# Two Transformer-style blocks in one kernel: identity turns at the start, four stages written in another order, the zero keys of four attention windows cut, and a split last store

## The chip, the cores and the metric

The kernel runs on one core of one Trainium2 chip. A core has TensorE (PE; its weight loads are shown as PEld), VectorE (DVE), ScalarE (ACT), GpSimd (POOL) and SyncE (SP, which only issues DMAs here). The time is device microseconds (us) of one execution, as the median over several executions; less is better. TensorE's clock has two levels, 1.2 and 2.4 GHz, and the profile's column PEclk says which share of 2.4 GHz was granted.

## The reference

Two blocks run one after the other on x of [1, 512, 1024] in float32. Cut to what matters:

```python
# first block
h = rms_norm(x, ln1_g);  z = h @ w_in            # 1024 -> 6656 columns
a = gelu(z_a); u, v = split(a)
v = layer_norm(v)                                 # over 512, with gain and bias
y_a = (u * chunked_spatial_gating(v, sg_w, sg_b)) @ w_a_out
c = p * sigmoid(g_lin)
c = causal_depthwise_conv(c, cv_w, cv_b)          # 31 taps, 512 channels
c = silu(layer_norm(c, cv_ln_g, cv_ln_b));  y_b = c @ w_b_out
y_c = stick_breaking_attention(q, k, vv) @ w_c_out   # 8 heads of 64
merged = gates[0] * y_a + gates[1] * y_b + gates[2] * y_c
x = x + merged @ w_out
up = causal_depthwise_conv(rms_norm(x, ln2_g) @ w_up, ffn_conv_w, ffn_conv_b)
x = x + (silu(gate) * val) @ w_down
# second block: a gated linear recurrence beside sliding-window attention
# (16 query heads, 4 key heads, window 128, blocks of 128, sinks; for the first
# block of queries the block of keys before it is all zeros and masked out)
merged = sigmoid(m_rnn) * (y_rnn @ w_rnn_out) + sigmoid(m_attn) * (y_attn @ w_attn_out)
x = x + merged @ w_o
out = rms_norm(x, final_norm_g)
```

## The kernel before, in words

Weights arrive on SP's queue in transfers of 1 MB into two STAGE buffers. Each transfer holds two "units". For a unit, ACT writes the rounded high part (`hi`, L585, WH) and DVE the rest (`lo`, L1030, WL), both in the format fp32r, into a ring of four slots; an activation is split the same way (XH, XL). A product is three matmuls of 512 columns, high by high, high by low, low by high, and a unit is 24 of them. PE takes the units in order (`unit(n)` waits for `hi_done` and `lo_done`); `hi(n + 4)` waits until PE is done with unit n. Every engine's program is one list written out by hand, and semaphores join the lists; PE, ACT and DVE each work strictly in order.

The places that this change touches, in order of time:

- **Start** (SP L430 to L441, ACT L605 to L620, DVE L1054 to L1085, PE L1749 to L1783). x comes in four token tiles (XTOK). PE turns each with 8 transposes into PSUM; DVE multiplies by the gain (`x_gain`, XG, L1058), ACT rounds (`x_high`, XH, L612) and copies (`x_copy`, XCM, L606), and DVE subtracts (`x_low`, XL, L1066). Unit 0 then goes over the four token tiles, unit 1 after it.
- **Second stage, units U_B** (DVE L1152 to L1262, PE L1842 on). DVE normalises the gate values VSG in four groups of three instructions (L1156 to L1161). After that it drains PSUM for unit i (`CPAD`, `TG`, L1239), and PE's unit i + 2 waits for the drain of unit i. Between the units PE does the steps of the stick-breaking attention (`stick_pe`), for which DVE does `pair_mask` (L1212) and `pair_scan` (L1225). The 124 instructions of the depthwise convolution (`taps`, CACC, L1180 and L1184) are dealt out over DVE's list.
- **Gate units of the last branch, `gates_first`** (p = 0 to 7; DVE L1303 to L1357, PE L1899 to L1917). DVE adds the four parts of CACC (L1319 to L1321, `c_sum`), and PE forms the mean with ONES after unit p = 2. Mean, variance, root and product follow, until BH and BL are there for the two "quad" units, which fill four PSUM banks. DVE then merges bank by bank (L1352, L1355).
- **Output projection, units U_D** (PE L1938 to L1944). The first unit waits for each of the eight parts MH and ML of the merged sum.
- **Windows of the second block** (PE L2056 to L2084, DVE L1517 on, ACT L863 and L874). 16 windows, each of 256 keys for 128 queries; for the windows with w % 4 == 0 the first 128 keys are zeros.
- **End** (DVE L1665 to L1677, SP L476 to L480): per token tile a drain, the sum of squares, a root, a reciprocal, one product over 1024 columns and one store of 512 KB.

## Time and profile before

| | us |
|---|---|
| median of 3 runs (lowest, highest) | 1326.31 (1323.57, 1326.85) |
| the profiled execution | 1323.74 |
| its span | 1321.8 |
| PE busy | 1298.2 (98%) |
| DVE busy | 844.5 (64%) |
| ACT busy | 609.5 (46%) |
| all DMA queues | 128.73 MB, mean 97 GB/s |

The span runs from the first to the last instruction that the profiler saw. In a row of the timeline the first number is the start in us from the span's start and the second the length; a matmul's length reaches over the next one's start, since matmuls are pipelined, so the distance between two starts is what one costs. The bracket at the end of a row is the idle time of that engine ahead of it and what ended it.

### The profile page before, as it was taken

To read this page: it belongs to the slowest core of one execution; us is meant where nothing else is said; L and a number is where in the kernel's file an instruction comes from. 1 tells how busy PE (TensorE), PEld (TensorE's weight loads), DVE (VectorE), ACT (ScalarE), POOL (GpSimd) and SP (SyncE) were. 2 spreads that over 40 slices of the span, in tenths; PEclk is the share of its full clock that TensorE was granted. 3 is DMA by queue.
4 is the path that set the end of the run, shared out by engine and by line. 5 is a ranking of instruction groups with operands and counts; after the bars stand their busy time and mean duration, and the time that the engine had idled before them with its cause. 6 is when DMAs were issued, how large, how long until landed. Compare 5 with 4: busy or idle time off the path is not lost.

```text
span 1321.8 us, 15645 instructions
## 1 busy us (share of the span) xinstructions
PE 1298.2 (98%) x5991; PEld 1046.0 (79%) x5991; DVE 844.5 (64%) x1110; ACT 609.5 (46%) x886; POOL 85.6 (6%) x70
## 2 busy tenths in 40 slices
PE   7999999999999999999999999999999999999997
PEld 6887777788777888888888888887877777778886
DVE  5458789889976776666665335435368878445534
ACT  6234467232263443333343224423389999544232
POOL 0000222000000200000000002100012220000000
PEclk9999999999999999999999999999999999999999
DMA  7432111422322322222222222422312221214211
GB/s 235 184 103 68 64 64 65 155 75 89 97 94 76 116 96 95 95 95 95 95 95 96 95 95 94 162 96 96 96 64 87 73 80 65 96 64 159 96 64 64
DMA packets 98282, 128.73 MB, mean 97 GB/s; under 512 B 2952, under 2 KB 80688, under 8 KB 97712
## 3 DMA queue, kind: packets, MB, share of 16 engines
q1 hardware_dynamic: 98208, 127.93, 28.7%
q8 instruction: 39, 0.64, 0.2%
q14 instruction: 19, 0.16, 0.0%
q10 hardware_dynamic: 16, 0.00, 0.0%
HBM read 121.63 MB, written 6.29 MB: 97 GB/s over the span
## 4 chain that ended last, share of the span: by engine, by line
PE 90%; DVE 7%; ACT 2%; DMA 1%; issue 1%; SPq 0%; DVEq 0%; ACTq 0%
PE PS L1683 87%; PE PS L1750 3%; DVE WL L1030 1%; ACT WH L585 1%; DMA STAGE<-in_w_in 1%; DVE QK L1132 0%; DVE CACC L1184 0%; DVE XL L1066 0%; DVE XG L1058 0%; DMA LNR<-in_ln_g 0%; DVE VSG L1160 0%; DVE MERG L1294 0%; DVE MERG L1355 0%; DVE MERG L1369 0%; DVE TMPY L1352 0%
## 5 line engine op out<-in xcount | busy, mean ns | idle before, releaser
L585 ACT ACTIVATE WH<-STAGE 128x1024 fp32r<-128x1024 f32 x214 | 225.8, 1057 | 489.5 <-PE PS L1683 473.6
L1030 DVE TENSOR_TENSOR WL<-STAGE,WH 128x1024 fp32r<-128x1024 f32 x214 | 276.3, 1293 | 228.3 <-ACT WH L585 227.8
L1683 PE MATMUL PS<-XH,WH 128*128 128x512 f32 x960 | 383.5, 399 | 2.4 <-DVE CPAD L1239 2.4
L1683 PE MATMUL PS<-XH,WL 128*128 128x512 f32 x960 | 375.6, 391 | 0.0
L1683 PE MATMUL PS<-XL,WH 128*128 128x512 f32 x960 | 375.4, 391 | 0.0
L1683 PEld LDWEIGHTS PS<-XH,WH 128*128 128x128 f32 x960 | 181.1, 189 | 45.1 <-issue 4.6
L1683 PEld LDWEIGHTS PS<-XL,WH 128*128 128x128 f32 x960 | 181.3, 189 | 38.7 <-issue 2.4
L1683 PEld LDWEIGHTS PS<-XH,WL 128*128 128x128 f32 x960 | 181.0, 189 | 38.3
L1683 PE MATMUL PS<-WH,XH 128*128 128x512 f32 x224 | 88.3, 394 | 1.1 <-DVE XL L1066 1.1
L1683 PE MATMUL PS<-WL,XH 128*128 128x512 f32 x224 | 87.3, 390 | 0.0
L1683 PE MATMUL PS<-WH,XL 128*128 128x512 f32 x224 | 87.3, 390 | 0.0
L1184 DVE SCALAR_TENSOR_TENSOR CACC<-CPAD,VEC,CACC 128x512 f32<-128x512 f32 x120 | 84.3, 760 | 0.1
L1403 DVE TENSOR_TENSOR UPB<-PS,RBC 128x512 f32<-128x512 f32 x44 | 30.3, 689 | 70.7 <-PE PS L1683 70.6
L1683 PE MATMUL PS<-FL,WH 128*128 128x512 f32 x176 | 68.5, 389 | 0.0
L1683 PE MATMUL PS<-FH,WH 128*128 128x512 f32 x176 | 68.5, 389 | 0.0
L1683 PE MATMUL PS<-FH,WL 128*128 128x512 f32 x176 | 68.5, 389 | 0.0
L510 POOL TENSOR_TENSOR SS<-SS,SQ 128x512 f32<-128x512 f32 x16 | 22.7, 1419 | 580.7 <-ACT SQ L594 580.7
L1683 PEld LDWEIGHTS PS<-WH,XH 128*128 128x128 f32 x224 | 42.2, 188 | 10.9 <-issue 1.1
L1683 PEld LDWEIGHTS PS<-WL,XH 128*128 128x128 f32 x224 | 42.2, 188 | 8.7 <-issue 0.2
L1683 PEld LDWEIGHTS PS<-WH,XL 128*128 128x128 f32 x224 | 42.1, 188 | 8.9
L791 ACT ACTIVATE YB<-UPB,VEC 128x512 f32<-128x512 f32 x44 | 35.3, 803 | 12.1 <-DVE UPB L1403 12.1
L1683 PEld LDWEIGHTS PS<-FH,WH 128*128 128x128 f32 x176 | 33.0, 188 | 6.9
(298 smaller groups left out, 1840.1 us busy)
## 6 DMA issues: line engine op xcount, KB each, us to landing
STAGE<-in_w_in SPq DMA_DIRECT2D x52, 1024.0 KB, 4.9
STAGE<-in_w_up SPq DMA_DIRECT2D x22, 1024.0 KB, 5.0
STAGE<-in_w_down SPq DMA_DIRECT2D x11, 1024.0 KB, 4.8
STAGE<-in_w_out SPq DMA_DIRECT2D x4, 1024.0 KB, 4.8
STAGE<-in_w_rnn_out SPq DMA_DIRECT2D x4, 1024.0 KB, 4.9
STAGE<-in_w_attn_out SPq DMA_DIRECT2D x4, 1024.0 KB, 4.7
STAGE<-in_w_o SPq DMA_DIRECT2D x4, 1024.0 KB, 4.9
XTOK<-in_x SPq DMA_DIRECT2D x4, 512.0 KB, 6.1
```

What stands on the lines that cost most here:

```text
L510: pool.tensor_tensor(SS[:], SS[:], SQ[:], ALU.add).then_inc(ss_added, 1)
L585: act.activation(ring(WH, n), staged(n), ACT.Copy).then_inc(hi_done, 1)
L791: act.activation(YB[:, r, :], UPB[:, r, 4:516], ACT.Identity, scale=VEC[:, bass.ds(V_FW[2] + c, 1)], bias=VEC[:, bass.ds(V_FB + c, 1)]).th ...
L1030: dve.tensor_tensor(ring(WL, n), staged(n), ring(WH, n).bitcast(F32), ALU.subtract)\
L1184: ins = dve.scalar_tensor_tensor(CACC[:, c, :], CPAD[:, c, 2 + j:2 + j + SEQ], col(V_CVW + KW * j + c), CACC[:, c, :], ALU.mult, ALU.add)
L1403: dve.tensor_tensor(UPB[:, r, 4:516], PS[:, r, :], RBC[:], ALU.mult)\
L1683: return pe.matmul(out_, lhsT, rhs, start=start, stop=stop, skip_group_check=True)
L1750: return pe.transpose(out_, in_, IDENT[:])
```

## The change

The list of changes, with where each stands:

1. Start: SP asks for x tile 0, then the first weights, then tiles 1 to 3. PE turns the identity 10 times before the gain row's transpose and 14 times between tile 0 and tile 1 (into a bank that nobody reads), turns tile 3 between unit 0 and unit 1 of tile 0, and does units 0 and 1 together for each token tile. ACT and DVE take the weights' parts ahead of the tiles' parts.
2. Second stage: the first drain stands ahead of the gate normalisation, which is dealt out in pairs of groups around the second drain; `pair_mask(0)` comes one step earlier. From i = 6 on a step has 4 taps in place of 3, and the last taps come earlier.
3. `gates_first`: sum, mean, squares, variance, root and product each stand one p earlier. The second quad unit goes bank by bank with a signal for each, and DVE merges on these signals, with `lo(U_D + 1)` behind the merges.
4. The first two units of the output projection are interleaved in halves of four parts.
5. Windows with w % 4 == 0 leave the 128 zero keys out of scores, mask, maximum, exponential, scaling, transposes and copy.
6. End: the left half is multiplied by the gain ahead of time and scaled by ACT, the right half by DVE, and each half is stored by itself.

The diff, cut:

```diff
+def first_key(w):
+
+    return 0 if w % TT else P
...
-            for t in range(2):
-                sp.dma_start(XTOK[:, t, :], xt[:, t, :]).then_inc(x_in[t], 16)
+            sp.dma_start(XTOK[:, 0, :], xt[:, 0, :]).then_inc(x_in[0], 16)
             for p, src in enumerate(transfers()):
                 kd, ncol = src.shape[1], src.shape[2]
                 if p == 1:
-                    for t in range(2, TT):
+                    for t in range(1, TT):
                         sp.dma_start(XTOK[:, t, :], xt[:, t, :]).then_inc(x_in[t], 16)
...
+            hi(0)
             x_high(0)
             x_copy(0)
-            hi(0)
+            hi(1)
             x_high(1)
             x_copy(1)
-            hi(1)
             x_high(2)
...
+            lo(0)
+            x_low(0)
             x_gain(1)
-            x_low(0)
-            lo(0)
+            lo(1)
             x_low(1)
             x_gain(2)
             x_gain(3)
             x_low(2)
...
-            dve.wait_ge(vg_sd, 1)
-            sd = SMALL[:, S_LN + 40:S_LN + 44]
-            link(dve.reciprocal(sd, sd))
-            for tt in range(TT):
+            def gate_norm(tt):
+                sd = SMALL[:, S_LN + 40:S_LN + 44]
+                if tt == 0:
+                    dve.wait_ge(vg_sd, 1)
+                    link(dve.reciprocal(sd, sd))
...
-            tap_order = [(c, j) for j in range(12) for c in (0, 1)]
-            tap_order += [(c, j + (12 if c < 2 else 0)) for j in range(CVK - 12) for c in range(KW)]
-            tap_order += [(c, j) for j in range(CVK - 12, CVK) for c in (2, 3)]
+            tap_order = [(c, j) for j in range(15) for c in (0, 1)]
+            tap_order += [(c, j + (15 if c < 2 else 0)) for j in range(CVK - 15) for c in range(KW)]
+            tap_order += [(c, j) for j in range(CVK - 15, CVK) for c in (2, 3)]
...
+                if i < 2:
+                    gate_norm(2 * i)
+                if i == 1:
+                    pair_mask(0)
+                if i < 2:
+                    gate_norm(2 * i + 1)
...
-                if 1 <= i < 13:
+                if 2 <= i < 13:
...
-                    taps(3)
+                    taps(3 if i < 6 else 4)
...
-                        taps(4)
-
+                        taps((4, 4, 4, 4, 6, 3)[r])
+
+            assert taps_done == KW * CVK
             for p in range(10):
-                dve.wait_ge(unit_done, U_C + 24 + p + 1)
+                if p < 9:
...
                 if p == 0:
-                    taps(4)
-                    assert taps_done == KW * CVK
-                if p == 1:
                     dve.wait_ge(c_tap, KW * CVK)
...
-                if p == 2:
+                if p == 1:
...
                 if p == 9:
                     for m in range(4):
+                        if m < 3:
+                            dve.wait_ge(quad_done, m + 1)
+                        else:
+                            dve.wait_ge(unit_done, U_C + 34)
                         dve.wait_ge(gs_ready, 16 + m + 1)
...
+            lo(U_D + 1)
             for m in range(4):
                 merged_low(m)
 
             for m in range(4):
                 if m < 3:
-                    dve.wait_ge(quad_done, m + 1)
+                    dve.wait_ge(quad_done, 3 + m + 1)
...
-                mask = AM[:, 1:3, :] if nb else AM[:, 0:3:2, :]
+                kb = first_key(w) // P
                 for par in range(2):
-                    dve.tensor_tensor(buf[:, par].rearrange("p i (b c) -> p i b c", b=2),
-                                      PS[:, 6 + par, :].rearrange("p (i b c) -> p i b c", i=2, b=2),
-                                      mask.unsqueeze(1).broadcast_to([P, 2, 2, P]),
+                    dve.tensor_tensor(buf[:, par].rearrange("p i (b c) -> p i b c", b=2)[:, :, kb:],
+                                      PS[:, 6 + par, :].rearrange("p (i b c) -> p i b c", i=2, b=2)[:, :, kb:],
+                                      AM[:, kb:, :].unsqueeze(1).broadcast_to([P, 2, 2 - kb, P]),
                                       ALU.add).then_inc(s2_mask, 1)
...
                 dve.wait_ge(s2_mask, 2 * w + 2)
-                link(dve.tensor_reduce(att(w, 0).rearrange("p (a b) -> p a b", a=2), buf[:], AX.X, ALU.max))
+                link(dve.tensor_reduce(att(w, 0).rearrange("p (a b) -> p a b", a=2),
+                                       buf[:, :, :, kb * P:], AX.X, ALU.max))
...
+                dve.wait_ge(fin_sq, t + 1)
+                v = XT2[:, t, 0:512]
+                dve.tensor_tensor(v, v, FG[:, 0:512], ALU.mult).then_inc(fin_gain, 1)
+            for t in range(TT):
...
-                link(dve.reciprocal(s_, s_))
-                dve.scalar_tensor_tensor(XT2[:, t, :], XT2[:, t, :], s_, FG[:], ALU.mult, ALU.mult)\
+                dve.reciprocal(s_, s_).then_inc(fin_rcp, 1)
+                dve.wait_ge(fin_rcp, t + 1)
+                dve.scalar_tensor_tensor(v, v, s_, FG[:, 512:1024], ALU.mult, ALU.mult)\
                    .then_inc(fin_ready, 1)
...
+            def turn_identity(n):
+
+                for _ in range(n):
+                    tr(PS[:, 6, 0:P], IDENT[:])
+
+            def x_turn(t):
...
+            pe.wait_ge(consts, 2)
+            turn_identity(10)
+            pe.wait_ge(ln_in, 16)
+            tr(PS[:, 7, 0:P], LNR[:]).then_inc(ln_t, 1)
+            x_turn(0)
+            turn_identity(14)
+            x_turn(1)
+            x_turn(2)
...
+            def first_units(t):
+                first_tile(t)
+                ts = slice(t * P, (t + 1) * P)
+                for n in (U_A, U_A + 1):
+                    if t == 0:
+                        unit(n)
+                        if n > U_A:
+                            x_turn(3)
+                    for k in range(2):
+                        kk = 2 * (n - U_A) + k
+                        last = split_mm(PS[:, t, :], XH[:, kk, ts], XL[:, kk, ts],
+                                        ring(WH, n)[:, k, :], ring(WL, n)[:, k, :], kk == 0, False)
+                    if t == TT - 1:
+                        last.then_inc(unit_done, 1)
+
+            for t in range(TT):
+                first_units(t)
 
...
-                    if p == 2:
+                    if p == 1:
                         pe.wait_ge(c_sum, 1)
                         pe.wait_ge(drained, DR_C + 32)
                         mm(PS[:, 4, :], ONES[:], TG1[:], True, True).then_inc(c_mean, 1)
-                    if p == 4:
+                    if p == 3:
                         pe.wait_ge(c_ssum, 1)
                         mm(PS[:, 5, :], ONES[:], TG0[:], True, True).then_inc(c_var, 1)
                 pe.wait_ge(c_cent, KW)
...
-                for u in range(2):
-                    quad_unit(U_C + 32 + u, u, 4, BH, BL, KW)
+                quad_unit(U_C + 32, 0, 4, BH, BL, KW)
+                n = U_C + 33
+                unit(n)
+                for m in range(4):
+                    for k in range(2):
+                        last = split_mm(PS[:, 4 + m, :], ring(WH, n)[:, k, m * P:(m + 1) * P],
+                                        ring(WL, n)[:, k, m * P:(m + 1) * P], BH[:, 2 + k, :],
+                                        BL[:, 2 + k, :], False, k == 1)
+                    last.then_inc(quad_done if m < 3 else unit_done, 1)
...
+            for h in range(2):
+                for m in range(2):
+                    if h == 0:
+                        pe.wait_ge(drained, DR_D - 7 + m)
+                        unit(U_D + m)
+                    for k in range(4 * h, 4 * h + 4):
+                        if m == 0:
+                            pe.wait_ge(mh_ready, k + 1)
+                            pe.wait_ge(ml_ready, k + 1)
+                        last = split_mm(PS[:, 4 + m, :], ring(WH, U_D + m)[:, k, :],
+                                        ring(WL, U_D + m)[:, k, :], MH[:, k, :], ML[:, k, :],
+                                        k == 0, k == KD - 1)
+                    if h:
+                        last.then_inc(unit_done, 1)
+            for m in range(2, KD):
                 pe.wait_ge(drained, DR_D - 7 + m if m < 4 else DR_D + m - 3)
-
-                def ready(k):
-                    pe.wait_ge(mh_ready, k + 1)
-                    pe.wait_ge(ml_ready, k + 1)
-                cm_unit(U_D + m, 4 + m % 4, MH, ML, 0, ready if m == 0 else None)
-
+                cm_unit(U_D + m, 4 + m % 4, MH, ML)
...
-                        last = mm(PS[:, 6 + par, idx * 256:idx * 256 + 256],
+                        last = mm(PS[:, 6 + par, idx * 256 + first_key(w):idx * 256 + 256],
                                   Q2T[rows_, 2 * g + idx, nb * P:(nb + 1) * P],
-                                  K2T[rows_, g, nb * P:nb * P + 256], True, True)
+                                  K2T[rows_, g, nb * P + first_key(w):nb * P + 256], True, True)
                 last.then_inc(qk2_done, 1)
...
-                for kb in range(2):
+                for kb in range(first_key(w) // P, 2):
...
+                        act.wait_ge(fin_rcp, t + 1)
+                        act.wait_ge(fin_gain, t + 1)
+                        act.activation(XT2[:, t, 0:512], XT2[:, t, 0:512], ACT.Copy,
+                                       scale=SMALL[:, S_FIN + t:S_FIN + t + 1]).then_inc(fin_left, 1)
...
+                sp.wait_ge(fin_left, t + 1)
+                sp.dma_start(ot[:, t, 0:512], XT2[:, t, 0:512]).then_inc(stored, 16)
                 sp.wait_ge(fin_ready, t + 1)
-                sp.dma_start(out.rearrange("o (t p) d -> p (o t) d", p=P)[:, t, :], XT2[:, t, :])\
-                  .then_inc(stored, 16)
-            sp.wait_ge(stored, 16 * TT)
+                sp.dma_start(ot[:, t, 512:1024], XT2[:, t, 512:1024]).then_inc(stored, 16)
```

PE's list at its beginning: before, and then of the change. XTOK are the x tiles, LNR the gain row, and the rows of WH, WL with XH, XL are unit 0.

```order
L1750 MATMUL PS<-IDENT,LNR 128x128
L1750 MATMUL PS<-IDENT,XTOK 128x128 x32
L1683 MATMUL PS<-WH,XH 128x512
L1683 MATMUL PS<-WL,XH 128x512
L1683 MATMUL PS<-WH,XL 128x512
```

```order
L1778 MATMUL PS<-IDENT 128x128 x10
L1778 MATMUL PS<-IDENT,LNR 128x128
L1778 MATMUL PS<-IDENT,XTOK 128x128 x8
L1778 MATMUL PS<-IDENT 128x128 x14
L1778 MATMUL PS<-IDENT,XTOK 128x128 x16
L1711 MATMUL PS<-WH,XH 128x512
L1711 MATMUL PS<-WL,XH 128x512
L1711 MATMUL PS<-WH,XL 128x512
```

The last 8 transposes of x moved behind the first six matmuls, and 24 turns of the identity are new.

DVE's list where the second stage begins: before, and then of the change. VSG are the gate values, CPAD the drains of units U_B + 0 and U_B + 1.

```order
L1150 TENSOR_SCALAR SMALL<-SMALL 128x4
L1154 RECIPROCAL SMALL<-SMALL 128x4
L1156 TENSOR_SCALAR VSG<-VSG,SMALL 128x512
L1160 TENSOR_TENSOR VSG<-VSG,SGLN 128x512
L1161 TENSOR_TENSOR VSG<-VSG,SGLN 128x512
...
L1161 TENSOR_TENSOR VSG<-VSG,SGLN 128x512
L1239 TENSOR_TENSOR CPAD<-PS,RBC 128x512
L1030 TENSOR_TENSOR WL<-STAGE,WH 128x1024
L1239 TENSOR_TENSOR CPAD<-PS,RBC 128x512
```

```order
L1160 TENSOR_SCALAR SMALL<-SMALL 128x4
L1250 TENSOR_TENSOR CPAD<-PS,RBC 128x512
L1166 RECIPROCAL SMALL<-SMALL 128x4
L1167 TENSOR_SCALAR VSG<-VSG,SMALL 128x512
L1171 TENSOR_TENSOR VSG<-VSG,SGLN 128x512
L1172 TENSOR_TENSOR VSG<-VSG,SGLN 128x512
...
L1172 TENSOR_TENSOR VSG<-VSG,SGLN 128x512
L1040 TENSOR_TENSOR WL<-STAGE,WH 128x1024
L1250 TENSOR_TENSOR CPAD<-PS,RBC 128x512
```

The first drain moved ahead of all twelve VSG instructions, the second ahead of six of them.

DVE's list at the end of the taps: before, and then of the change, from the last MERG row on. CACC x4 are taps, GS drains of the units p = 0 and 1, and the two TG names the sum that PE's mean needs.

```order
L1294 TENSOR_TENSOR MERG<-MERG,TMPY 128x512
L1184 SCALAR_TENSOR_TENSOR CACC<-CPAD,VEC,CACC 128x512 x4
L1311 TENSOR_TENSOR GS<-PS,RBC 128x512
L1030 TENSOR_TENSOR WL<-STAGE,WH 128x1024
L1184 SCALAR_TENSOR_TENSOR CACC<-CPAD,VEC,CACC 128x512 x4
L1311 TENSOR_TENSOR GS<-PS,RBC 128x512
L1030 TENSOR_TENSOR WL<-STAGE,WH 128x1024
L1319 TENSOR_TENSOR TG_77<-CACC 128x512
L1320 TENSOR_TENSOR TG_94<-CACC 128x512
L1321 TENSOR_TENSOR TG_77<-TG_77,TG_94 128x512
```

```order
L1311 TENSOR_TENSOR MERG<-MERG,TMPY 128x512
L1330 TENSOR_TENSOR GS<-PS,RBC 128x512
L1040 TENSOR_TENSOR WL<-STAGE,WH 128x1024
L1336 TENSOR_TENSOR TG_77<-CACC 128x512
L1337 TENSOR_TENSOR TG_94<-CACC 128x512
L1338 TENSOR_TENSOR TG_77<-TG_77,TG_94 128x512
```

Eight taps, one drain and one WL row no longer stand between the last merge and the sum.

## Rows read from the trace of the kernel before

**Rows 1.** Waits of PE: what waited for what, us in total, times, longest.

```profile
PE PS L1683 <- DVE TG L1321: 2.8, 1, 2.8
PE PS L1683 <- ACT MH L769: 2.8, 3, 1.0
PE PS L1683 <- DVE CPAD L1239: 2.4, 1, 2.4
PE PS L1683 <- DVE XL L1066: 1.1, 2, 0.6
PE PS L1683 <- ACT II L905: 0.8, 1, 0.8
```

**Rows 2.** Timeline of the start, PE and DVE.

```profile
9.81 0.48 PE L1750 MATMUL PS<-IDENT,XTOK 128*128 128x128 f32 x1 [1.52 <-DMA XTOK<-in_x]
13.14 0.75 PE L1683 MATMUL PS<-WH,XH 128*128 128x512 f32 x1
19.42 2.36 DVE L1030 TENSOR_TENSOR WL<-STAGE,WH 128x1024 fp32r<-128x1024 f32 x2 [0.40 <-ACT WH L585]
```

**Rows 3.** The first weight transfer, issued at 1.71: time to landing.

```profile
DMA to landing us min/median/max: 6.8/6.8/6.8
```

**Rows 4.** Busy time by stretch: start:end length, PE, PEld, DVE, ACT, POOL, PEclk, DMA share, GB/s.

```profile
9.80:13.10 3.30, 3.29 (x16) 3.29 (x17) 3.08 (x3) 3.30 (x5) 0.00 (x0) 1.00 1.04 384
122.90:126.40 3.50, 3.49 (x8) 2.84 (x9) 3.50 (x5) 0.00 (x0) 0.00 (x0) 0.51 0.00 0
364.57:372.00 7.43, 7.43 (x26) 5.80 (x25) 3.52 (x5) 3.08 (x5) 0.00 (x0) 0.77 0.24 90
```

**Rows 5.** Timeline where the second stage begins, PE and DVE.

```profile
114.31 0.18 DVE L1154 RECIPROCAL SMALL<-SMALL 128x4 f32<-128x4 f32 x1 [1.80 <-ACT SMALL L661]
122.17 0.68 DVE L1239 TENSOR_TENSOR CPAD<-PS,RBC 128x512 f32<-128x512 f32 x1
122.91 0.79 PE L1683 MATMUL PS<-XH,WH 128*128 128x512 f32 x1 [2.43 <-DVE CPAD L1239]
```

**Rows 6.** Waits of DVE from 128 to 240 us, as in rows 1.

```profile
DVE TG L1239 <- PE PS L1683: 6.3, 4, 3.3
DVE WL L1030 <- ACT WH L585: 5.7, 11, 1.3
```

**Rows 7.** Timeline around the sum of the convolution, ACT, DVE and PE.

```profile
344.95 1.06 ACT L585 ACTIVATE WH<-STAGE 128x1024 fp32r<-128x1024 f32 x1 [4.38 <-PE PS L1683]
350.39 1.06 ACT L585 ACTIVATE WH<-STAGE 128x1024 fp32r<-128x1024 f32 x1 [4.38 <-PE PS L1683]
353.05 2.74 DVE L1184 SCALAR_TENSOR_TENSOR CACC<-CPAD,VEC,CACC 128x512 f32<-128x512 f32 x4
360.10 0.68 DVE L1311 TENSOR_TENSOR GS<-PS,RBC 128x512 f32<-128x512 f32 x1
364.01 1.13 PE L1683 MATMUL PS<-TG,ONES 128*128 128x512 f32 x2 [2.84 <-DVE TG L1321]
```

**Rows 8.** Timeline of PE at the first unit of the output projection.

```profile
420.71 0.39 PE L1683 MATMUL PS<-MH,WL 128*128 128x512 f32 x1
422.10 0.47 PE L1683 MATMUL PS<-MH,WH 128*128 128x512 f32 x1 [1.00 <-ACT MH L769]
```

**Rows 9.** Timeline of PE: a window's transposes and scores, with the rows behind them.

```profile
1120.56 1.03 PE L1750 MATMUL PS<-IDENT,S2A 128*128 128x128 f32 x8
1121.35 0.48 PE L1683 MATMUL PS<-BHR,WH 128*128 128x512 f32 x1
...
1128.00 1.14 PE L1683 MATMUL PS<-K2T,Q2T 64*128 64x256 f32 x8
1129.07 0.50 PE L1683 MATMUL PS<-BHR,WH 128*128 128x512 f32 x1
```

**Rows 10.** The end on DVE, and the last store's time to landing.

```profile
1317.51 1.28 DVE L1676 SCALAR_TENSOR_TENSOR XT<-XT,SMALL,FG 128x1024 f32<-128x1024 f32 x1
...
DMA to landing us min/median/max: 2.6/2.6/2.6
```

More of the change, by code:

```diff
@@ L529, in _ @@
             pool.wait_ge(unit_done, U_G)
-            pool.memset(AM[:, 0, :], -BIG).then_inc(gchain, 1)
-            pool.memset(AM[:, 1:3, :], 0.0).then_inc(gchain, 1)
-            n += 2
+            pool.memset(AM[:], 0.0).then_inc(gchain, 1)
+            n += 1
             pool.wait_ge(gchain, n)
-            pool.affine_select(out=AM[:, 1, :], in_=AM[:, 1, :], compare_op=ALU.is_gt, fill=-BIG,
+            pool.affine_select(out=AM[:, 0, :], in_=AM[:, 0, :], compare_op=ALU.is_gt, fill=-BIG,
                                base=0, pattern=[[1, P]], channel_multiplier=-1).then_inc(consts, 1)
-            pool.affine_select(out=AM[:, 2, :], in_=AM[:, 2, :], compare_op=ALU.is_ge, fill=-BIG,
+            pool.affine_select(out=AM[:, 1, :], in_=AM[:, 1, :], compare_op=ALU.is_ge, fill=-BIG,
                                base=0, pattern=[[-1, P]], channel_multiplier=1).then_inc(consts, 1)
-            pool.memset(K2T[:, :, 0:P], 0.0).then_inc(consts, 1)
             pool.memset(UP2[:, :, 0:4], 0.0).then_inc(consts, 1)
@@ L1081, in _ @@
             x_low(2)
-            lo(1)
             x_low(3)
@@ L1750, in tr @@
                 return pe.transpose(out_, in_, IDENT[:])
-            pe.wait_ge(consts, 2)
-            pe.wait_ge(ln_in, 16)
-            tr(PS[:, 7, 0:P], LNR[:]).then_inc(ln_t, 1)
-            for t in range(TT):
+            def turn_identity(n):
+                for _ in range(n):
+                    tr(PS[:, 6, 0:P], IDENT[:])
+            def x_turn(t):
                 pe.wait_ge(x_in[t], 16)
```

41 lines of the change are left out of this document (24 added, 17 removed).

## The prediction, made before the kernel was run

> **What bounds the kernel now.** I read the page first: PE is busy for 1298.2 of 1321.8 us, and no other engine is above 64%. So only PE's 23.6 us of idle time, the time it runs below full clock, and work taken off its list can be worth anything. The waits of PE come next [rows 1]: 2.8 us for the sum TG, 2.8 us in three pieces for MH, 2.4 us for the drain CPAD, 1.1 us for XL and 0.8 us for II; the reader is to see that each is one place, not a pattern. Then the timeline at those places, for what the wait is made of, and the busy time by stretch [rows 4] for the clock: behind the waits for CPAD and TG the granted clock is 0.51 and 0.77, so each of them is followed by matmuls at the lower of the two levels, 1.2 GHz. What a wait costs is its length and that stretch together.
>
> Two prices recur. A unit of 24 matmuls at full clock takes 5.44 us, the distance of the two WH rows that each follow a finished unit [rows 7]; that is 0.227 us per matmul. A transpose takes (1121.35 - 1120.56)/8 = 0.10 us there [rows 9], but (13.14 - 9.81)/16 = 0.21 us at the start [rows 2].
>
> **The change part by part.**
>
> *Start.* The column PEclk says 1.00 for 9.80 to 13.10 [rows 4], yet the 16 transposes in it go at 0.21 us, half the pace of those at 1120 us; so PE starts at the lower level and the column does not show it. The Trainium skill warns of this (TensorE: Matmul & The Clock Gate, section "Seeing it yourself"): the clock's trace events have been seen to be unreliable and should be cross-checked against durations. The rows bear that out, and by the column alone the identity turns could gain nothing.
>
> Before, the first matmul starts at 13.14 [rows 2]. Units 0 and 1 are 48 matmuls or 10.9 us; with the waits for XL, 1.1 us, and the slow first matmuls and restarts, about 0.9, unit 1 ends at 26.0. After, the first weights stand ahead of x tile 1. They were issued at 1.71 and landed 6.8 later, at 8.5 [rows 3]; tile 2, the 0.5 MB right behind, let PE go at 9.81 [rows 2], so 0.5 MB is 1.3 us, and the weights land at 7.2. The 10 turns fill PE from about 1.6 to 3.7, tile 0 is turned when it is there, as before, and the 14 turns take 3.0 us slow or 1.4 fast, to 9.4 at the latest, which delays tile 1 (there at 8.5) by at most 0.9 us. From there DVE sets the pace, with ten operations of about 1.15 us from start to start (two WL take 2.36 [rows 2], and XG and XL have as many elements). ACT: WH 7.2 to 8.3, XH to 9.3, XCM to 10.3. DVE: WL 8.4 to 9.5, XL to 10.7. PE starts unit 0 at 10.75, does six matmuls, turns tile 3 and waits for the WL of unit 1 at 13.0. XL of tile 2 comes at 17.7, and from there PE has two tiles of 24 matmuls in all: 17.7 + 5.44 = 23.2. The gain is 26.0 - 23.2 = 2.8 us. Bounds: 0 if the ten DVE operations in the new order take as long as before, 3.5 if PE never waited behind 10.75 (10.75 + 10.9 + 0.9 for tile 3). I take 2.8.
>
> *Second stage.* PE is done with the scores at 122.91 - 2.43 = 120.48 and waits 2.43 us, since DVE drains CPAD at 122.17, behind the twelve VSG operations [rows 5]. Then 8 matmuls take 3.5 us [rows 4] where 1.8 would do: 1.7 lost. After, both drains come sooner: the first ahead of the root's wait, the second at 119.5, behind two groups of (122.17 - 114.31)/4 = 1.97 us and one WL. PE needs only the first. The saving is 2.43 + 1.7 = 4.1 us; I take 4.0, since the first matmul behind an attention step is a little slow at any clock. What is late next: from 114.31 DVE needs four groups, a drain of 0.68, a mask of the same size and a WL of 1.15 until the last VSG, 124.7, and 1.3 for WT, 126.0; PE asks for both after its unit and the next scores, 120.48 + 5.44 + 0.9 = 126.8. It fits with 0.8 us to spare. Six steps then have one tap more, 6 x 0.69 = 4.1 us (a row of four taps is 2.74 [rows 7]). DVE's own waits in that stretch, 6.3 + 5.7 us over eleven steps [rows 6], cover it; when the cover is gone PE waits. Bounds 0 and 4.0; I take 4.0.
>
> *The sum.* PE starts p = 0 at 344.7 and has finished p = 1 two units later, at 355.6 [rows 7]. DVE ends the merges at 353.05. From the drain at 360.10 to PE's start at 364.01 it needs 3.91 us for drain, WL and three additions [rows 7]; the same after 353.05 gives 356.96. So a wait of 1.4 us stays where 3.0 was (with the restart), a gain of 1.6. Behind the wait of 2.84 us, 24 matmuls take 7.43 us at 0.77 [rows 4], 2.0 more than 5.44. Waits of 1.00 us do not bring the clock down [rows 8], one of 2.43 does [rows 5]; 1.4 is nearer to the first. I take 1.6 + 1.9 = 3.5; bounds 1.6 and 4.9. The rest of the chain (squares, variance, root) moves with the sum, and PE asks for BL six units later, as it did five units later before, so nothing is late there.
>
> *Output projection.* The three waits are 2.8 us [rows 1]; between 420.71 and 422.10 is 1.39 for one matmul of 0.23, so a wait of 1.00 costs 1.16 [rows 8], and the three 3.3. After, the second unit's first half gives 12 matmuls, 2.7 us, of work that needs only parts 0 to 3, and DVE's merges start about 4 us sooner. All 3.3 goes. The WL that now stands behind the merges is ready at about 410, and PE needs it at 419. Bounds 2.8 and 3.3.
>
> *Windows.* Four of sixteen lose half their columns. Transposes: 4 of 8, 0.40 of 0.79 us. Scores: the eight rows of 256 columns take 1.07 us (1128.00 to 1129.07) [rows 9]; half the columns can save at most 0.53 and at least 0, and I take 0.45, near the half, as the columns of the transposes are paid in full. That is 4 x 0.85 = 3.4 us off PE's list. The wait of 0.8 for II [rows 1] ends a chain through window 0's mask, maximum, exponentials and copy, all halved, by some 2 us in sum; PE comes 0.85 sooner, so the wait goes too: 4.2. Bounds 0.8 (the scores save nothing and the chain does not move) and 4.5. The mask's and the memset's work on POOL was hidden and is worth nothing.
>
> *End.* Half the columns are scaled on DVE while ACT does the rest: 1.28 becomes about 0.7 [rows 10], and the copy that the store needs is 256 KB instead of 512, against a second issue on SP. The last landing took 2.6 us [rows 10]. I take 0.6; bounds 0.2 and 1.2. The Trainium skill (DMA: Bandwidth & Descriptors, "Anatomy of one DMA") gives about 2.0 us plus the bytes by 436 GB/s, measured on GpSimd's path: estimated by it, 3.2 for the old store, more than the 2.6 here, and 0.6 less for the half. With 0.3 for the product and the issues, the end would gain 0.9 by it instead of 0.6.
>
> **Sum**: 2.8 + 4.0 + 3.5 + 3.3 + 4.2 + 0.6 = 18.4 us. The profiled execution had 1323.74 (span 1321.8 and 1.9 around it), so one like it would have 1305.3. It lies near the lowest of the runs, 1323.57; the median is 2.6 above it. I expect the median in the middle of such a spread, 1.3 above: **1306.6**.
>
> **The rivals.**
> - *The clock falls again behind the 1.4 us.* For it: 2.43 was enough. Against: three waits of about 1 us within 5 us were not. Then 1.9 more: 1308.5.
> - *DVE falls behind in the second stage.* It is nearly full there, and the extra taps are 4.1 us. If its own waits do not cover them, PE's scores wait for the sigmoid, which waits for DVE's mask, and the 4.0 is given back: 1310.6.
> - *The start gives nothing*, as DVE's ten operations, or the weights' landing, set the end of unit 1: 1309.4.
> - *It becomes slower.* One mechanism: with PE 4 us sooner, each of the ten steps from 130 to 215 us ends in a wait for DVE's mask. Small waits add; from 18.4/10 = 1.8 us a step on, all is lost, and waits of that size are near the 2.43 that brought the clock down for 1.6. With 2.4 + 1.6 at each of ten steps, 40 us, it would be 1346; with waits of 2.1 us alone, 1328. Against it: DVE has about 1.1 us of its own waits in a step now [rows 6], and no wait of PE stands in that stretch [rows 1].
> - *The change does not do what it says*: the identity turns end before the clock rises. They cost nothing then, since they lie in waits for the DMAs; that is within the start's bounds.
>
> **How the numbers follow.** Forecast 0.60; clock again 0.13; DVE behind 0.11; start gives nothing 0.10; smaller misses of several terms together, near 1312 to 1318, 0.03; slower 0.03. The range 1302 to 1313 holds the first four with their spread; the lower end is the upper bounds of start, sum, windows and end (0.7 + 1.4 + 0.3 + 0.6 more) with the spread's 1.3. A measurement here tells 0.3%, 4.0 us, from no change, that is below 1322.3 for faster. Only the last two cases come near it: faster 0.96, same 0.02, slower 0.02.
>
> **What would show it.** In the profile after: PE's first matmul of unit 0 near 10.8 and the end of unit 1 near 23; no wait for CPAD and a clock of 1.00 in the stretch behind; a wait for TG of about 1.4 with the clock still at 1.00; no waits for MH; scores of window 0 in about 0.6 instead of 1.07 and no wait for II; two stores per tile, and a last product of 0.69 us. A new line of PE waiting for ACT's GB or BT between 120 and 220 us would prove the forecast wrong, as would a median above 1313.

## The result, and the profile after

The change took 17.1 us off the median: 1307.83 us (1307.77 to 1308.16, four runs) against 1324.94 (1323.45 to 1326.85, four runs of the kernel before beside it), a ratio of 0.9871 with a 95% interval of 0.9857 to 0.9884. I had forecast 1306.6 in a range of 1302 to 1313. The profiled execution of the changed kernel took 1308.16 with a span of 1306.4; the one of before took 1323.74 with 1321.8. So from profile to profile 15.6 us went, 15.4 of them in the span, where my sum had 18.4.

First line of part 1 of the changed kernel's page, and then its waits of PE (what waited for what, us in total, times, longest):

```profile
PE 1292.2 (99%) x5999; PEld 1042.2 (80%) x5999; DVE 842.0 (64%) x1114; ACT 608.1 (47%) x890; POOL 85.3 (7%) x68
```

```profile
PE PS L1778 <- POOL ONES L504: 1.6, 1, 1.6
PE PS L1711 <- DVE TG L1338: 1.2, 1, 1.2
PE PS L1711 <- ACT BT L677: 0.9, 1, 0.9
PE PS L1778 <- DVE KDUP L1522: 0.8, 1, 0.8
PE PS L1778 <- ACT AT L686: 0.8, 1, 0.8
PE PS L1711 <- ACT II L911: 0.5, 1, 0.5
```

Of the five waits in [rows 1], MH, CPAD and XL are gone, TG fell from 2.8 to 1.2 and II from 0.8 to 0.5. Two are new, for BT and for AT, both in the second stage: the line of which I had said that it would prove the forecast wrong. It did so for one step of it. (The 1.6 for ONES is the start: PE now waits for the identity and then turns it, in the time in which it waited 4.4 us for the gain row LNR before.)

What each place gave is read from the start of one and the same PE instruction in both timelines. Before, at six places:

```profile
53.77 0.59 PE L1683 MATMUL PS<-SS,ONES 128*128 128x512 f32 x1
141.16 0.70 PE L1683 MATMUL PS<-QKT 64*128 64x512 f32 x2
220.87 0.38 PE L1750 MATMUL PS<-IDENT,BT 128*128 128x128 f32 x2
416.47 0.39 PE L1683 MATMUL PS<-MH,WH 128*128 128x512 f32 x1
469.13 0.59 PE L1683 MATMUL PS<-SS,ONES 128*128 128x512 f32 x1
1314.79 0.39 PE L1683 MATMUL PS<-WH,M2L 128*128 128x512 f32 x1
```

And after, the same six:

```profile
51.20 0.59 PE L1711 MATMUL PS<-SS,ONES 128*128 128x512 f32 x1
134.49 0.70 PE L1711 MATMUL PS<-QKT 64*128 64x512 f32 x2
216.10 0.30 PE L1778 MATMUL PS<-IDENT,BT 128*128 128x128 f32 x1 [0.76 <-ACT AT L686]
408.50 0.39 PE L1711 MATMUL PS<-MH,WH 128*128 128x512 f32 x1
457.46 0.59 PE L1711 MATMUL PS<-SS,ONES 128*128 128x512 f32 x1
1299.36 0.39 PE L1711 MATMUL PS<-WH,M2L 128*128 128x512 f32 x1
```

The lead is 2.57, then 6.67, 4.77, 7.97, 11.67 and 15.43 us (at the last matmul), and at the span's end 15.4. The steps between are what each place gave:

| place | forecast | from trace to trace |
|---|---|---|
| start | 2.8 | 2.57 |
| second stage, drains first | 4.0 | 4.10 |
| the same stage, up to 216 us | 0 | -1.90 |
| the sum | 3.5 | 3.20 |
| output projection | 3.3 | 3.70 |
| windows, with the wait for II | 4.2 | 3.76 |
| end | 0.6 | 0.0 |
| in all | 18.4 | 15.4 |

At the two places where the clock was low before [rows 4], the busy time by stretch of the changed kernel (us, then busy us of PE, PEld, DVE, ACT, POOL with their instructions, PEclk, DMA share, GB/s) has it at full level; PE's wait ahead of the second was 1.25 us:

```profile
117.90:121.40 3.50, 3.50 (x18) 2.90 (x17) 3.36 (x7) 1.99 (x3) 0.00 (x0) 1.00 0.00 0
352.10:359.60 7.50, 7.40 (x31) 5.80 (x32) 4.87 (x8) 3.81 (x7) 0.00 (x0) 1.00 0.42 142
```

In windows with w % 4 == 0 the transposes and the scores are about halved; the rows of window 0 and of window 4 after, against the full ones in [rows 9] (eight transposes in 0.79 from start to start, eight scores in 1.07):

```profile
954.07 0.60 PE L1778 MATMUL PS<-IDENT,S2A 128*128 128x128 f32 x4
994.55 0.72 PE L1711 MATMUL PS<-K2T,Q2T 64*128 64x128 f32 x8
```

The row of eight full scores in [rows 9] has a length of 1.14, so halving the columns took 0.42 off; my 0.45 was near.

### The profile page after: what moved, and what is told of

Same layout as the page of the kernel before. It is cut to its first block, busy times and chain, and to the rows that moved or that the text cites. A ratio compares the mean times of both kernels' runs of the same rounds, so it can differ in the third digit from the quotient of the medians.

```text
span 1306.4 us, 15673 instructions
## 1 busy us (share of the span) xinstructions
PE 1292.2 (99%) x5999; PEld 1042.2 (80%) x5999; DVE 842.0 (64%) x1114; ACT 608.1 (47%) x890; POOL 85.3 (7%) x68
## 4 chain that ended last, share of the span: by engine, by line
PE 91%; DVE 5%; ACT 2%; DMA 1%; issue 1%; SPq 0%; ACTq 0%; DVEq 0%
PE PS L1711 88%; PE PS L1778 3%; DVE WL L1040 1%; ACT WH L590 1%; DMA STAGE<-in_w_in 1%; DMA XTOK<-in_x 1%; DVE QK L1142 0%; DVE CACC L1195 0%; DVE RS L1236 0%; DVE MERG L1311 0%; DVE TMPY L1307 0%; DVE VATT L1124 0%; DVE UC L1572 0%; DVE VSG L1124 0%; ACT BT L677 0%
## 5 line engine op out<-in xcount | busy, mean ns | idle before, releaser
L1040 DVE TENSOR_TENSOR WL<-STAGE,WH 128x1024 fp32r<-128x1024 f32 x214 | 280.3, 1312 | 217.2 <-ACT WH L590 216.6
L1711 PEld LDWEIGHTS PS<-FL,WH 128*128 128x128 f32 x176 | 33.0, 188 | 6.9
```

The lines of the kernel that those rows point to most:

```text
L1040: dve.tensor_tensor(ring(WL, n), staged(n), ring(WH, n).bitcast(F32), ALU.subtract)\
L1711: return pe.matmul(out_, lhsT, rhs, start=start, stop=stop, skip_group_check=True)
```

## The experiments

Times are medians; the changed kernel itself gave 1307.83 on one chip and 1307.92 (1307.82 to 1308.05) on another, beside the last three kernels. Its expectation there was:

> The changed kernel itself, beside the next three on one chip: 1307.8, spread under 1 us, while the kernel before spreads over 3 us.

That held. The kernel before gave 1324.8 to 1325.5 beside all of them, spread over 3.1 to 3.8 us. Ratios are to it. "Less" and "more" are against 1307.83 for the changed kernel, and against 1307.92 for the three kernels that ran beside its second measurement. From trace to trace the start alone moves by up to 0.6 us, with the arrival of the first data, so a lead read at one place holds only when the lead ahead of it is taken off.

**Who fills VectorE in the second stage.** The wait for BT (longest 0.95 in its row at 205.65) means that ACT had not read the scores out of PSUM; ACT waited for DVE's mask, and the mask stood behind a long WL. Four experiments.

*Taps back.*

```diff
-                    taps(3 if i < 6 else 4)
+                    taps(3)
-                        taps((4, 4, 4, 4, 6, 3)[r])
+                        taps(((4, 4, 4, 4, 6, 3) if b + q == 0 else (5, 5, 5, 5, 6, 3))[r])
```

> The changed kernel, but with 3 taps in every step from i = 4 on, as before, and the six moved taps dealt out one at a time over the units of the later quads of the third stage. Theory (the added taps fill VectorE): the two new waits of TensorE, for BT at 205.7 us (0.95) and for AT at 216.1 us (0.76), which cost 1.11 + 0.92 = 2.0 us, go, and the last scores before 217 us start 2.0 us earlier, 1307.8 - 2.0 = 1305.8. Rival (the waits come from TensorE being 4.1 us earlier than before, and VectorE and GpSimd are in each other's way whatever the taps): the waits stay, 1307.8.

1306.31 (1306.19 to 1306.63), 1.5 us less; ratio 0.9856 (0.9841 to 0.9871). The wait for BT is gone, that for AT is 0.4 instead of 0.8. By 216 us the trace is 1.10 earlier although its start was 0.27 later, so the stage gave 1.4. That is most of the loss of 1.9, and not all: between the theory and its rival. What is left has a cause of its own, in the step ahead of the wait (DVE, then POOL):

```profile
206.57 2.36 DVE L1210 TENSOR_TENSOR UU<-UU,TG 128x512 f32<-128x512 f32 x1 [0.16 <-ACT TG L716]
```

```profile
206.56 1.82 POOL L531 TENSOR_TENSOR BT<-BT,RS 128x768 f32<-128x768 f32 x1 [5.86 <-DVE RS L1236]
```

UU<-UU,TG takes 0.66 in the same step of the changed kernel. Here it is 1.7 longer, ACT's WH waits 2.42 for it, and WL, mask and sigmoid come behind WH. The next experiments show what stretches it.

*Drains alone.* The kernel before with this and the rest of that stage's edit:

```diff
                 dve.tensor_tensor(dst, PS[:, i % 2, :], RBC[:], ALU.mult).then_inc(drained, 1)
+                if i < 2:
+                    gate_norm(2 * i)
```

> The kernel before with only the change to the drains, the gate normalisation and the first mask of the second stage. Theory (taps fill VectorE): with 3 taps a step the whole 4.1 us of the CPAD wait and the low clock behind it is kept, 1324.9 - 4.1 = 1320.8, and TensorE waits for neither BT nor AT. Rival (TensorE's lead is the cause): 2.0 of it is given back, 1322.9, with the two waits of some 0.8 us there.

1320.90 (1318.48 to 1323.04, nine runs), ratio 0.9968 (0.9958 to 0.9978), 4.6 us less than before. In the trace it is 4.1 (3.5 earlier at 141 us, from a start that was 0.6 later), and no wait of PE at all between 117 and 230 us. With three taps a step the whole 4.1 stays. The rival falls.

*Mask first.* What is long about WL? DVE's timeline in a step of the changed kernel, then POOL's:

```profile
182.40 0.66 DVE L1250 TENSOR_TENSOR TG<-PS,RBC 128x512 f32<-128x512 f32 x1
182.99 2.53 DVE L1040 TENSOR_TENSOR WL<-STAGE,WH 128x1024 fp32r<-128x1024 f32 x1
185.44 0.42 DVE L1223 TENSOR_TENSOR PS<-PS,MMIN 128x256 f32<-128x256 f32 x1
```

```profile
182.62 1.82 POOL L531 TENSOR_TENSOR BT<-BT,RS 128x768 f32<-128x768 f32 x1 [6.52 <-DVE RS L1236]
```

WL takes 1.22 where nothing runs beside it, and here 2.53: of the 1.45 us that it lies beside POOL's product it lost 1.31. The scan that ends ahead of the drain releases the product, so in the four steps from 174 to 203 us the WL starts beside it. The Trainium skill has this (GPSIMD Engine Reference, section "Specifications"): GpSimd's way into SBUF is shared with VectorE, and they contend where a VectorE instruction has two SBUF inputs. The trace agrees, and also where one input is in PSUM: the drain beside it keeps its 0.66.

Which of the two loses goes by which began first. In the rows above the product was there first, in those of the taps' experiment by 0.01 us, and VectorE lost. At 208.92 of the changed kernel VectorE was first:

```profile
208.92 0.66 DVE L1210 TENSOR_TENSOR UU<-UU,TG 128x512 f32<-128x512 f32 x1
```

```profile
209.14 2.15 POOL L531 TENSOR_TENSOR BT<-BT,RS 128x768 f32<-128x768 f32 x1 [6.52 <-DVE RS L1236]
```

Here UU keeps its 0.66, and the product takes 2.15 instead of 1.82. In the trace of the drains alone both begin at 209.42; UU takes 0.69 and the product 2.38. So the last step of that trace was spared the collision that the taps' experiment has. The experiment moves WL:

```diff
-                lo(U_B + i + 4)
+                if i < 6:
+                    lo(U_B + i + 4)
                 if 2 <= i < 13:
                     pair_mask(i - 1)
                 tg_mult(i - 1)
+                if i >= 6:
+                    lo(U_B + i + 4)
```

> The changed kernel, but from i = 6 on VectorE's subtraction WL stands behind the mask and the gate product instead of ahead of them. Theory (VectorE is full, and its operations that read two SBUF operands run at about half pace while GpSimd's product BT<-BT,RS runs): the PSUM drain and the mask then lie beside GpSimd's product, WL takes 1.2 to 1.9 us instead of 2.5 to 2.7, the mask comes over 1 us earlier in each step, and the waits for BT and AT go: 1307.8 - 1.9 = 1305.9. Rival (the mask now waits for the scores, and VectorE stands idle ahead of it): nothing gained, 1307.8 or up to 1 us more.

1306.00 (1305.84 to 1306.20), 1.8 us less, with all the added taps in place; ratio 0.9855 (0.9839 to 0.9872). Both waits are gone. The same step, DVE and then POOL:

```profile
181.74 0.67 DVE L1250 TENSOR_TENSOR TG<-PS,RBC 128x512 f32<-128x512 f32 x1
182.32 0.42 DVE L1223 TENSOR_TENSOR PS<-PS,MMIN 128x256 f32<-128x256 f32 x1
182.65 1.68 DVE L1210 TENSOR_TENSOR UU<-UU,TG 128x512 f32<-128x512 f32 x1
184.25 1.21 DVE L1040 TENSOR_TENSOR WL<-STAGE,WH 128x1024 fp32r<-128x1024 f32 x1
```

```profile
181.96 1.82 POOL L531 TENSOR_TENSOR BT<-BT,RS 128x768 f32<-128x768 f32 x1 [6.19 <-DVE RS L1236]
```

Drain and mask, which work on PSUM, pass beside the product at their own pace. VectorE's UU<-UU,TG, both inputs in SBUF, takes the collision (1.68 instead of 0.68), and a WL of 1.21 follows. The mask starts 0.58 us behind the drain's start instead of 3.04, and with it the sigmoids.

*Half of POOL's product.* Half of the products BT<-BT,RS is left out, the four taps stay.

```diff
-                pool.tensor_tensor(b, b, RS[:, :, 0:STEP_W[s % 3]], ALU.mult).then_inc(a_ready, 1)
+                b, rs = b[:, 0], RS[:, 0, 0:STEP_W[s % 3]]
+                pool.tensor_tensor(b, b, rs, ALU.mult).then_inc(a_ready, 1)
```

> The changed kernel, with GpSimd's product BT<-BT,RS of the stick-breaking steps over one of its two halves; the other half of the products is left out. Its 4 taps per step stay. Theory (GpSimd's product stretches VectorE's WL): the WL beside it falls from 2.5 to about 1.9 us, the waits for BT and AT go or shrink to under 0.5 us in sum, 1306.1. Rival (WL is long for a reason of its own, the taps alone fill VectorE): WL stays at 2.5, and the waits stay, 1307.8.

1306.16 (1305.90 to 1306.24), 1.7 us less; ratio 0.9856 (0.9839 to 0.9872). DVE's WL, then POOL's product in that step:

```profile
182.28 1.73 DVE L1041 TENSOR_TENSOR WL<-STAGE,WH 128x1024 fp32r<-128x1024 f32 x1
```

```profile
181.93 1.00 POOL L532 TENSOR_TENSOR BT<-BT,RS 128x384 f32<-128x384 f32 x1 [6.53 <-DVE RS L1237]
```

With POOL at 1.00, WL loses 0.5, and both waits are gone. So the cause is shown from both sides: the taps and the collision together fill DVE, and taking away either one brings most of the loss back.

**The turns of the identity.**

```diff
-            turn_identity(10)
...
-            turn_identity(14)
```

> The changed kernel without the 24 turns of the identity. Theory (the turns raise the clock): the transposes of tiles 1 and 2 and the first matmuls go at 0.21 and 0.45 us instead of 0.10 and 0.23; tile 2 is turned 1.0 us later, the six first matmuls take 1.3 more, the third turn of x 0.8 more; with what VectorE's pace hides of it, unit 1 ends 1.5 to 3 us later: 1309.3 to 1310.8. Rival (VectorE's ten operations alone set the start): no change, 1307.8.

1308.47 (1308.19 to 1308.64), 0.55 to 0.64 more than the changed kernel; ratio 0.9873 (0.9858 to 0.9888). PE's timeline without the turns, and then with them:

```profile
8.40 3.57 PE L1778 MATMUL PS<-IDENT,XTOK 128*128 128x128 f32 x16 [1.78 <-DMA XTOK<-in_x]
11.73 0.48 PE L1711 MATMUL PS<-WH,XH 128*128 128x512 f32 x1
12.04 0.40 PE L1711 MATMUL PS<-WL,XH 128*128 128x512 f32 x1
```

```profile
8.53 1.09 PE L1778 MATMUL PS<-IDENT,XTOK 128*128 128x128 f32 x8 [0.37 <-DMA XTOK<-in_x]
9.81 1.09 PE L1778 MATMUL PS<-IDENT,XTOK 128*128 128x128 f32 x8 [0.19 <-DMA XTOK<-in_x]
11.05 0.47 PE L1711 MATMUL PS<-WH,XH 128*128 128x512 f32 x1
```

The turns do raise the clock: tiles 1 and 2 go at half the price, and the first matmul starts 0.68 earlier. Then the changed kernel waits 0.40 before tile 3, and without turns the matmuls are at full level almost at once, so behind tile 3 only 0.13 of it is left. My expectation of 1.5 to 3 us is refuted, and its rival is nearly right. By this pair of traces the turns gave 0.1 us, by the medians, on different chips, about 0.6; the other 2.0 to 2.4 of the start's 2.6 us are the order of tiles and weights.

**The sum ahead of the last merges.** DVE's three additions, moved in front of the four merges of the last quad:

```diff
+                        if r == 5 and b == 1 and q == 1:
+                            dve.wait_ge(c_tap, KW * CVK)
+                            link(dve.tensor_tensor(TG1[:], CACC[:, 0, :], CACC[:, 1, :], ALU.add))
...
                         if r == 5:
                             for m in range(4):
```

> The changed kernel, with the three additions of the convolution's parts ahead of the last four merges instead of behind them, the first drain and a WL. Theory (the wait of 1.25 us for TG is the length of what stands on VectorE between the merges and the sum): it goes with its restart, 1307.8 - 1.4 = 1306.4, and no wait of TensorE takes its place, since the merges, 2 us later, free their banks ahead of the mean. Rival (TensorE then waits for the merges, which free bank 4): the wait changes its name and half of it or all stays, 1307.1 to 1307.8.

1306.51 (1306.43 to 1306.65), 1.3 less; ratio 0.9859 (0.9842 to 0.9875). No wait for TG is left, the mean starts at 350.92 instead of 352.20, and nothing took its place. So the wait lay in what VectorE had to do ahead of the sum, the last merges, one drain and one WL, and the merges themselves can wait.

**The output projection.** Two experiments. First PE's interleaving of units alone taken back:

```diff
-            for h in range(2):
-                for m in range(2):
...
+            for m in range(KD):
+                pe.wait_ge(drained, DR_D - 7 + m if m < 4 else DR_D + m - 3)
...
+                cm_unit(U_D + m, 4 + m % 4, MH, ML, 0, ready if m == 0 else None)
```

> The changed kernel, with the first two units of the output projection one after the other as before, while the merges bank by bank stay. Theory (the signals per bank are what took the waits for MH away; VectorE has the last low part at 412.5 us, and TensorE would ask for it at 413.3): no change, 1307.8. Rival (the interleaving is needed): waits for MH of 0.5 to 2 us in sum come back, 1308.3 to 1310.

1308.16 (1308.00 to 1308.44), ratio 0.9871 (0.9855 to 0.9888), with no wait of PE between 380 and 460 us. The interleaving is worth at most 0.3 us. Then the signals per bank taken back as well, and with them the place of one WL, which stands ahead of the merges again:

```diff
-                        if m < 3:
-                            dve.wait_ge(quad_done, m + 1)
-                        else:
-                            dve.wait_ge(unit_done, U_C + 34)
                         dve.wait_ge(gs_ready, 16 + m + 1)
...
-            lo(U_D + 1)
             for m in range(4):
                 merged_low(m)
```

> The changed kernel with the merges at p = 9 without signals per bank, the WL of U_D + 1 ahead of them, and the first two projection units one after the other, all as before. Theory (the waits for MH cost their length and restart, and at times the clock falls behind them, which is a part of the 3 us by which the kernel before spreads): three waits for MH of 2.1 to 2.8 us in sum, +3.3 to +3.8, so a median of 1311.1 to 1311.6 with single runs up to 2 us above. Rival (the waits cost 3.3 and never touch the clock; the spread of before comes from the waits for CPAD and TG alone): 1311.1 with a spread under 0.7 us.

1312.25, 4.3 us more, with runs at 1311.59, 1311.77, 1312.73 and 1313.72; ratio 0.9902 (0.9887 to 0.9917). The profiled one was the slowest. Its PE, and the stretch behind:

```profile
412.23 0.47 PE L1704 MATMUL PS<-MH,WH 128*128 128x512 f32 x1 [0.80 <-ACT MH L774]
414.16 0.75 PE L1704 MATMUL PS<-MH,WH 128*128 128x512 f32 x1 [1.00 <-ACT MH L774]
414.71 0.63 PE L1704 MATMUL PS<-ML,WH 128*128 128x512 f32 x1
415.14 0.63 PE L1704 MATMUL PS<-MH,WL 128*128 128x512 f32 x1
```

```profile
416.30:422.00 5.70, 5.70 (x16) 4.46 (x17) 4.52 (x6) 3.80 (x5) 0.64 (x1) 0.59 0.25 79
```

From 414.16 on a matmul costs 0.43 instead of 0.23. These are the waits that in the trace of before, with 0.81 and 1.00, left the clock alone [rows 8]. The trace of the drains alone shows the fall too: behind its waits of 0.80 and 1.01 for MH the matmuls from 417 to 423 us cost 0.43. And the other way round: in that same trace the wait of 2.84 us for TG, as long as in [rows 7], is followed by the full level, where [rows 4] has 0.77. PE's row and its stretch there:

```profile
360.46 1.12 PE L1690 MATMUL PS<-TG,ONES 128*128 128x512 f32 x2 [2.84 <-DVE TG L1328]
```

```profile
361.00:371.00 10.00, 10.00 (x45) 8.10 (x44) 6.92 (x11) 4.77 (x7) 0.00 (x0) 1.00 0.23 78
```

So whether the clock falls behind such waits differs between executions. A single wait of 1.25 us for TG, which ten of the traces have, cost no clock in any of them. All kernels that still have the waits for MH or CPAD spread over 2.1 to 4.6 us; the others, ten kernels with four or five runs each, over at most 0.7. The rival, that the waits for MH never touch the clock, is refuted. The signals per bank were not tried apart from the place of that WL: of the 5.5 us by which the merges start later without them (400.24 for 394.74), the WL is 1.15.

**The windows back.**

```diff
-    return 0 if w % TT else P
+    return 0
```

(with the mask for it)

> The changed kernel with all sixteen windows over 256 keys, as before. Theory (only what TensorE no longer does counts, as the wait for II varies by 0.5 us between runs with no change there): 4 x 0.85 = 3.4 comes back, 1311.2. Rival (the chain through window 0 also held II, as I forecast): 4.2 comes back, 1312.0, with a wait for II of 0.8.

1312.10 (1311.86 to 1312.57), 4.2 more; ratio 0.9903 (0.9887 to 0.9918), and the wait for II is 0.7. My forecast's 4.2 was right here, and the theory of 3.4 wrong. The wait for II itself is 0.5 in the first trace of the changed kernel and absent in the second, with the same code: hence 3.76 by the first pair of traces, and 4.2 by the medians.

**One store per tile.**

```diff
+                sp.wait_ge(fin_left, t + 1)
                 sp.wait_ge(fin_ready, t + 1)
-                sp.dma_start(ot[:, t, 512:1024], XT2[:, t, 512:1024]).then_inc(stored, 16)
+                sp.dma_start(ot[:, t, :], XT2[:, t, :]).then_inc(stored, 16)
```

> The changed kernel, with the halves scaled apart on ScalarE and VectorE as it does, but one store of 512 KB per tile behind both. Theory (the second issue and its own landing eat what the shorter product gives): the tail behind the last matmul is 7.0 us with two stores and becomes 6.6 with one, 1307.4. Rival (the smaller last store lands earlier, as I forecast): the tail becomes longer, 7.3, 1308.1.

1307.78 (1307.51 to 1307.96): no difference; ratio 0.9867 (0.9852 to 0.9882). The tail from the start of the last matmul to the span's end is 7.33 here, 7.04 and 7.35 in the two traces of the changed kernel, 7.01 before: neither theory. The stretch of the last store, first before, then with one store and the halved product (queue: packets, MB, share; and issue to landing):

```profile
q1 hardware_dynamic: 144, 0.52, 32.3%
issues: line engine op xcount, KB each, median us to landing
out<-XT SPq DMA_DIRECT2D x1, 512.0 KB, 2.6
```

```profile
q14 instruction: 1, 0.01, 1.2%
issues: line engine op xcount, KB each, median us to landing
out<-XT SPq DMA_DIRECT2D x1, 512.0 KB, 3.4
```

The product is shorter by 0.53 (0.75 for 1.28), the issue comes 0.5 earlier, and the same 512 KB land 0.8 later behind it. What differs is one packet of instructions on the DMA engines at that moment, of 8 KB: it is in this stretch in all twelve traces that descend from the changed kernel, and in neither that descends from before. The times of the single packets explain the delay. The instructions take one engine 0.76 us, from 1303.36 to 1304.12. The store is spread over 16 engines, eight packets of 4 KB on each. Before, all 16 end their shares within 0.15 us. With one store, 15 end from 1304.52 to 1304.67, and the last one's eight packets start only at 1304.12, where the instructions end, and run to 1305.36. The stretch from 1304.7 to 1305.4, five packets and 5.8% of 16 engines, that is one engine at work:

```profile
q1 hardware_dynamic: 5, 0.02, 5.8%
```

In eleven of the twelve traces the last engine ends 0.5 to 0.7 us behind the other 15. The twelfth is that of the next kernel, where the packet comes only as the store ends and the last engine is 0.1 behind; its tail is 7.07 all the same, and why stays open.

**Three edits together**, on the changed kernel: mask first, sum early, and

```diff
+                        if t == TT - 1:
+                            act.wait_ge(fin_left, TT)
+                            act.dma_start(out.rearrange("o (t p) d -> p (o t) d", p=P)[:, t, 0:512],
+                                          XT2[:, t, 0:512]).then_inc(stored, 16)
```

> The changed kernel with three edits more: from i = 6 on the mask and the gate product ahead of WL (measured alone -1.8), the sum ahead of the last four merges (alone -1.3), and the left half of the last token tile stored from ScalarE's own queue right behind its scaling, beside the right half on SyncE's. Theory (the gains add, and the second issue of 0.4 us was on the path of the end): 1307.8 - 1.8 - 1.3 - 0.4 = 1304.3. Rival (the store from another queue gives nothing, since the landing of the later half sets the end and varies by 0.2): 1304.7.

1304.28 (1304.02 to 1304.48, five runs), 3.6 us under the changed kernel on the same chip; ratio 0.9843 (0.9829 to 0.9856). The two gains on DVE's list add, 1.8 and 1.3. For the store 0.3 to 0.5 remains, by which of the two medians of the changed kernel the first two are counted, and the tail is 7.07, within what tails differ by. The Trainium skill (DMA: Bandwidth & Descriptors, section "Issuing engines are not separate DMA queues") says that issuing from two engines saves only the time to issue; nothing here speaks against it.

## Why the prediction was right, and where it was not

The total was right to 1.2 us and the sign with it. Four of the six terms held within 0.5 us of the trace; the second stage missed by 1.8 and the end by 0.6. These misses and one on the median cancel in part, so that the total came so near is luck.

- *Start*: 2.8, measured 2.57. Unit 0 began at 11.05 for my 10.75, and unit 1 ended at 23.50 for 23.2 (before, at 26.07 for 26.0). I had DVE set the pace up to the XL of tile 2. It did so up to the WL of unit 1, the wait of 0.40 at 13.05. Behind that PE never waited: XL of tile 2 was there at 17.65, as forecast at 17.7, but PE came to that tile by its own list only at 18.06. The rival of no gain falls. That the turns matter hardly was within my bounds, but I gave it as a mere possibility.
- *Second stage*: the step that failed is "DVE's own waits in that stretch, 6.3 + 5.7 us over eleven steps [rows 6], cover it". The 4.1 came, and 1.9 of it went again: that is my rival "DVE falls behind", chance 0.11, with half its price. I counted 4.1 us of taps against 12 us of DVE's waits over eleven steps. But a wait saved up in one step is no cover in another. And the cover was needed twice: a WL that waits for nothing starts right behind the drain, where POOL's product has just begun. The four rows of WL in the steps ahead of 205 us took 2.13, 1.95, 1.23 and 2.27 before and 2.56, 2.53, 2.73 and 2.57 after, 2.8 us more in all, for which my sum had no term. In the trace of before seven of eleven rows were already longer than 1.3, and I had read only the idle time ahead of them. One of them:

```profile
181.06 2.13 DVE L1030 TENSOR_TENSOR WL<-STAGE,WH 128x1024 fp32r<-128x1024 f32 x1 [0.35 <-ACT WH L585]
```

- *The sum*: 3.5, measured 3.20; the wait of 1.25 for my 1.4, with the clock up. The rival of a second fall did not occur. But the 1.9 for the clock in this term was a draw of one execution, as the drains alone show.
- *Output projection*: 3.3, measured 3.7 in the trace. By medians all that was taken back here cost 4.3, since the clock can fall behind these waits too. I took [rows 8] as proof that it doesn't. And the reason was half wrong: the signals per bank, with the WL behind the merges, do nearly all of it, and the interleaving at most 0.3.
- *Windows*: 4.2, measured 3.8 by the first pair of traces, where 0.5 of the wait for II was left, and 4.2 by medians.
- *End*: 0.6, measured 0.0 in the first pair of traces. Product and issue went as worked out; the landing did not: behind the one store it was 3.4 us for my 2.6, since one DMA engine had instructions to bring first.
- *From profile to median*: I added 1.3 because before spreads. The changed kernel's median is 0.3 below its profiled run, and its runs are within 0.4: the waits behind which the clock varies are gone. So 2.8 us too much in the sum, 1.6 too much for the median.

## What to carry to other kernels

Cover for added work must be in the same step as the work, and is counted with the collisions there: list what runs on GpSimd beside each VectorE instruction with two SBUF inputs, see which of the two begins first, and put instructions on PSUM beside GpSimd's instead. Waits of TensorE of 2.4 to 2.8 us, or three of about 1 us close together, cost their length always and the clock sometimes, so one trace cannot price them. The spread of the runs can tell that such waits are there, and removing them takes more off the median (17.1 us here) than off the best run (15.7). Of a bundle of edits, those that start something sooner (signals per bank, drains first, the order of the first transfers) and the one that removes work (the windows) carried the gain, and those that fill time gave little (identity turns 0.1 to 0.6 us, interleaved units at most 0.3).

## What the runs showed of the hardware

- A VectorE operation with two SBUF inputs that begins while GpSimd's product runs nearly stops until the product ends: 1.31 us lost of 1.45 beside it (WL), 1.0 of 1.13 (UU<-UU,TG), 1.7 of 1.8 (UU<-UU,TG with the taps back). Where it began first, it kept its 0.66 us and the product was the longer one, 2.15 for 1.82. An operation with one input in PSUM, 0.66 us, lost nothing.
- TensorE's clock behind the same waits: at the lower level behind 2.84 us in one execution (0.77) and at the full one in another (1.00); at the lower behind two waits of 0.8 and 1.0 us in two executions (matmuls of 0.43 us for 0.23) and at the full one in a third.
- Without any turns the clock is up at the second matmul of 512 columns; PE had by then turned 8 and 16 transposes at the low level, with a pause of 1.78 us between.
- The last store of 512 KB landed in 2.6 us, or in 3.4 where an instruction packet of 8 KB held one of the 16 DMA engines for 0.76 us ahead of its share: the store is done when its last engine is.
